# First two expert pairs gathered together as float32r halves, and three expert weight items asked for earlier

## The reference

```python
grp_prob = jax.nn.softmax((t @ w_grp) + b_grp, axis=-1)
g_prob, g_sel = lax.top_k(grp_prob, 1)                     # one of 4 groups
exp_logits = ((t @ w_rtr) + b_rtr).reshape(-1, N_GROUPS, EXP_PER_GROUP)
in_grp = jnp.take_along_axis(exp_logits, g_sel[:, :, None], axis=1)[:, 0]
e_prob, e_sel = lax.top_k(jax.nn.softmax(in_grp, axis=-1), 2)   # two of its 8 experts
gate = g_prob * e_prob / jnp.sum(e_prob, -1, keepdims=True)
...
hid = jax.nn.silu(jnp.einsum('td,edf->tef', t, w1)) * jnp.einsum('td,edf->tef', t, w3)
y = jnp.einsum('tef,efd->td', hid * combine[..., None], w2)
```

## Time and profile before

| | |
|---|---|
| median of 3 runs | 1316.39 us (1315.42 to 1318.79) |
| profiled execution, its own time | 1315.97 us |
| its span | 1314.2 us |
| TensorE busy | 97% of the span |
| mean granted TensorE clock | 0.992 of full |
| layer 0, experts | about 583 to 812 us of the span |
| layer 1, experts | about 1078 to 1302 us of the span |

### The profile page before, as it was taken

The page is one execution under the profiler, slowest core; times in us unless marked ns, Lnnn a source line. Parts: engine busy times, 40 slices in busy tenths (PEclk is TensorE's granted clock), DMA queues, the critical chain, the costliest instruction groups (busy, mean ns, idle before and its releaser), DMA issues.

```text
span 1314.2 us, 19284 instructions
## 1 busy us (share of the span) xinstructions
PE 1278.9 (97%) x7509; PEld 824.9 (63%) x7509; DVE 562.1 (43%) x1226; ACT 485.4 (37%) x1062; POOL 115.3 (9%) x167
## 2 busy tenths in 40 slices
PE   8999999999999999999999998999999999999996
PEld 7888588885888877454344443788887554444432
DVE  3325223262577584342232215678485242222224
ACT  3346333462663236212223323563235412223232
POOL 0000000000014331000000000004422000000000
PEclk9999999999999999989999999999999999999999
DMA  9753162332421234759999999231132859999994
GB/s 368 149 176 121 40 266 97 129 111 81 166 106 63 77 111 161 288 198 362 418 420 422 421 416 404 78 128 67 65 128 98 321 213 398 420 420 422 422 420 189
DMA packets 48847, 307.51 MB, mean 234 GB/s; under 512 B 5897, under 2 KB 6409, under 8 KB 16752
## 3 DMA queue, kind: packets, MB, share of 16 engines
q1 hardware_dynamic: 43760, 288.61, 55.3%
q0 software_dynamic: 3200, 8.16, 2.8%
q10 hardware_dynamic: 1792, 9.43, 1.9%
HBM read 301.17 MB, written 8.59 MB: 236 GB/s over the span
## 4 chain that ended last, share of the span: by engine, by line
PE 85%; DVE 10%; ACT 4%; issue 1%; DMA 0%; DVEq 0%; ACTq 0%; SPq 0%
PE ps L1136 25%; PE ps L1812 17%; PE ps L1839 9%; PE ps L1401 4%; PE ps L1176 4%; PE ps L1881 2%; PE ps L1902 2%; PE ps L1108 2%; PE ps L1621 1%; PE ps L1144 1%; DVE projT L2755 1%; DVE small L2754 1%; PE ps L1821 1%; PE ps L1611 1%; DVE projT L2746 1%
## 5 line engine op out<-in xcount | busy, mean ns | idle before, releaser
L1136 PE MATMUL ps<-hT,ring 128*128 128x272 f32 (+1 forms) x1840 | 437.1, 391 | 0.6 <-ACT hT L1995 0.6
L1136 PEld LDWEIGHTS ps<-hT,ring 128*128 128x128 f32 x1840 | 343.7, 191 | 66.2 <-issue 8.0
L1812 PE MATMUL ps<-ring,arena 128*64 128x512 f32 x416 | 139.3, 600 | 0.0
L3110 DVE TENSOR_TENSOR xo<-ps,xo 128x512 fp32r<-128x512 f32 x64 | 42.9, 689 | 99.5 <-ACT xo L2427 99.4
L3227 POOL TENSOR_TENSOR arena<-projT,cst 32x272 f32<-32x272 f32 x104 | 71.5, 687 | 114.2 <-DVE projT L2733 101.1
L1812 PE MATMUL ps<-projT,arena 128*64 128x512 f32 x240 | 80.0, 597 | 0.0
L3101 DVE TENSOR_TENSOR arena<-arena,ps 128x256 f32<-128x256 f32 x32 | 13.5, 421 | 140.6 <-ACT arena L2414 140.0
L1812 PEld LDWEIGHTS ps<-ring,arena 128*64 128x64 f32 x416 | 40.4, 137 | 51.9 <-issue 51.0
L2412 ACT ACTIVATE arena<-ps 128x256 f32<-128x256 f32 x32 | 12.3, 384 | 138.7 <-PE ps L1812 138.7
L2154 ACT ACTIVATE projT<-ps 128x272 f32<-128x272 f32 x68 | 27.0, 397 | 90.8 <-PE ps L1136 85.2
L1401 PE MATMUL ps<-ring,projT 128*128 128x512 f32 x128 | 56.6, 596 | 0.0
(11 more groups left out here) (511 smaller groups left out, 2026.6 us busy)
## 6 DMA issues: line engine op xcount, KB each, us to landing
ring<-experts SPq DMA_DIRECT2D x72, 1024.0 KB, 16.5
ring<-w_in SPq DMA_DIRECT2D x62, 1024.0 KB, 5.0
projT<-experts SPq DMA_DIRECT2D x48, 1024.0 KB, 15.8
arena<-experts SPq DMA_DIRECT2D x22, 1024.0 KB, 12.3
prm<-experts SPq DMA_DIRECT2D x22, 1024.0 KB, 16.0
ring<-w_out SPq DMA_DIRECT2D x16, 1024.0 KB, 4.8
spare<-experts SPq DMA_DIRECT2D x12, 1024.0 KB, 14.5
lent<-experts SPq DMA_DIRECT2D x8, 1024.0 KB, 10.2
```

The source lines that it names most:

```text
L1136: mm = pe.matmul(ps[:, chunk_bank(blk, l, j), 0:ncols], w[:, j % 2, k, :], hT[:, k, T - ncols:T], start=(k == 0), stop=(k == KC - 1))
L1812: mm = pe.matmul(ps[64 * e:64 * e + 64, 0, :], xg[:, 4 * h + k, i % 2, 64 * e:64 * e + 64], w[e][:, k // 2, 512 * (k % 2):512 * (k % 2) + ...
L3110: v.tensor_tensor(low, ps[:, 4 + half, :], high, ALU.subtract).then_inc(s("pair_rows_copied"), 1)
```

## The change

Pairs 0 and 1 are gathered by `gather_two(0, 0)` and `gather_two(0, 1)` before the first `up_half`; `gather_pair` is gone. Its second half goes to PSUM banks 6 and 7, so it does not wait for the copy of the first. VectorE builds `psel` in two parts of 256 columns rather than 128 and 384, and splits the first group's rows right behind, in two halves of 512 columns. `keep_busy` gets one more matmul of 512 columns in each layer. SyncE no longer waits for `rows_fetched` at item 14.

```diff
@@ SyncE
                     if j == 7 + MORE_SLOTS + ITEMS_WO:
                         sp.wait_ge(layer_normed, normed_at[l, 1, 2, 1])
-                        sp.wait_ge(rows_fetched, 16 * (GROUPS * l + 1))
@@
-        def together(i):
-            return i >= 2
         def copies_of(i):
-            return 2 * (min(i + 1, 2) + max(i // 2, 0))
+            return 2 * (i // 2 + 1)
+        def gather_bank(i, half):
+            return 6 if i == 0 and half else 2
@@ TensorE
-                    return group + 3 if group else 1 if q == 0 else 2
+                    return group + 3 if group else 1 if q < 2 else 2
...
-                def gather_pair(i):
-                    q = i % PAIRS_A_GROUP
-                    pe.wait_ge(s("pairs_selected"), selected(0, q))
-                    if i == 0:
-                        pe.wait_ge(rows_fetched, 16 * (GROUPS * l + 1))
-                    else:
-                        pe.wait_ge(s("pair_tokens_copied"), copies_of(i - 1))
-                    for k in range(KC):
-                        mm = pe.matmul(ps[:, 2 + k // 4, (k % 4) * P:(k % 4 + 1) * P], xrows[:, k * P:(k + 1) * P],
-                                       whole(psel)[:, 2 * q:2 * q + 2, :], start=True, stop=True)
-                        if k % 4 == 3:
-                            mm.then_inc(s("pair_gathered"), 1)
                 def gather_two(i, half):
                     q = i % PAIRS_A_GROUP
                     if half == 0:
                         pe.wait_ge(s("pairs_selected"), selected(i // PAIRS_A_GROUP, q))
-                        pe.wait_ge(s("rows_split"), i // PAIRS_A_GROUP + 1)
                         if q == 2:
                             pe.wait_ge(s("pairs_turned_copied"), i // PAIRS_A_GROUP + 1)
-                    pe.wait_ge(s("pair_tokens_copied"), copies_of(i - 1) + half)
+                    pe.wait_ge(s("rows_split"), i // PAIRS_A_GROUP + 2 if i else half + 1)
+                    if i:
+                        pe.wait_ge(s("pair_tokens_copied"), copies_of(i - 1) + half)
...
                 def experts_grouped():
-                    gather_pair(0)
+                    gather_two(0, 0)
+                    gather_two(0, 1)
...
                         if i == 0:
                             gate_slots(0)
-                            gather_pair(1)
...
-                keep_busy(4, *([256] if l < LAYERS - 1 else [384, 512, 512, 384]))
+                keep_busy(4, *([256, 512] if l < LAYERS - 1 else [384, 512, 512, 384, 512]))
@@ ScalarE: every pair of pairs by the 128x1024 copy, pairs 0 and 1 too
-                            if i == 0 or i % 2 and i + 1 < PAIRS:
+                            if i % 2 and i + 1 < PAIRS:
                                 tokens_in(i + 1)
@@ VectorE
-                        chosen(0, 2).then_inc(s("pairs_selected"), 1)
-                        chosen(2, PER_GROUP).then_inc(s("pairs_selected"), 1)
+                        chosen(0, 4).then_inc(s("pairs_selected"), 1)
+                        chosen(4, PER_GROUP).then_inc(s("pairs_selected"), 1)
...
                     v.wait_ge(rows_fetched, 16 * (GROUPS * l + g + 1))
-                    if g == 0:
-                        v.wait_ge(s("pair_gathered"), 4)
-                    VP(v.tensor_copy(rows_high, xrows))
-                    v.tensor_tensor(rows_low, xrows, rows_high, ALU.subtract).then_inc(s("rows_split"), 1)
+                    parts = [slice(0, 512), slice(512, D)] if g == 0 else [slice(0, D)]
+                    for c in parts:
+                        VP(v.tensor_copy(rows_high[:, c], xrows[:, c]))
+                        v.tensor_tensor(rows_low[:, c], xrows[:, c], rows_high[:, c], ALU.subtract).then_inc(s("rows_split"), 1)
...
                         hidden(i)
-                        if i == 0:
-                            split_rows(0)
...
                 select_pairs(0)
+                split_rows(0)
```

More of the change, by code:

```diff
@@ L1880, in gather_two @@
                         for part, rows in enumerate((rows_high, rows_low)):
-                            mm = pe.matmul(ps[:, 2 + k // 2, (k % 2) * 2 * P:(k % 2 + 1) * 2 * P], rows[:, c],
+                            mm = pe.matmul(ps[:, gather_bank(i, half) + k // 2, (k % 2) * 2 * P:(k % 2 + 1) * 2 * P], rows[:, c],
                                            psel[:, 2 * q:2 * q + 4, :], start=(part == 0), stop=(part == 1))
@@ L1885, in turn_pairs @@
                 def turn_pairs(g):
-                    pe.wait_ge(s("pairs_selected"), selected(g, 1))
+                    pe.wait_ge(s("pairs_selected"), selected(g, 2))
                     for q in range(PAIRS_A_GROUP):
@@ L2391, in tokens_in @@
                             a.wait_ge(s("pair_gathered"), copies_of(i) - 1 + half)
-                            if together(i):
-                                a.activation(xg[:, 4 * half:4 * half + 4].rearrange("p (b k) c n -> p b (k c n)", b=2),
-                                             ps[:, 2:4, :], ACT.Copy)\
-                                    .then_inc(s("pair_tokens_copied"), 1)
-                            else:
-                                a.activation(xg[:, 4 * half:4 * half + 4, i % 2, :],
-                                             ps[:, 2 + half, :].rearrange("p (k n) -> p k n", k=4), ACT.Copy)\
-                                    .then_inc(s("pair_tokens_copied"), 1)
+                            b = gather_bank(i, half)
+                            a.activation(xg[:, 4 * half:4 * half + 4].rearrange("p (b k) c n -> p b (k c n)", b=2),
+                                         ps[:, b:b + 2, :], ACT.Copy)\
+                                .then_inc(s("pair_tokens_copied"), 1)
                     def turned_in():
```

## The result

Over 22 runs of each in turn, the changed kernel took 1319.99 us in the median (1316.06 to 1324.09), the kernel before 1316.63. The ratio is 1.0025, 95% interval 1.0016 to 1.0033: **3.3 us slower**. That lies inside the predicted range and under the 3.9 us taken as the bound of "the same", but it is surely not the -0.2 us of the sum. The profiled execution took 1317.62 us, the second fastest of the 22; its span is 1315.8.

What follows compares the result with a forecast made beforehand. The prediction took TensorE, busy 97% of the span, as the bound. Layer 0 at -1.15 and layer 1 at +0.95 gave -0.2 us together: median 1316.2 us, range 1312.8 to 1320.8.

Steps and rivals of the forecast that it cites:

- layer 0, start: Layer 0's experts through `up_half(0, 0)`: added filling shortens the low-clock stretch to about 3 us, -0.8 us.
- layer 0, pair 1: Layer 0 ahead of `up_half(1, 0)`: gather removed, most of its time becomes idle, -0.35 us.
- layer 1, start, by the gather: Layer 1's start through `up_half(0, 0)`: longer filling and gather in halves start it later, +1.3 us.
- layer 1, start, by the items: Layer 1's store and fetch of rows beside three early weight items: shared evenly, cost 0.
- layer 1, pair 1: Layer 1 ahead of `up_half(1, 0)`: gather removed, most of its time becomes idle, -0.35 us.
- Part 3: TensorE ahead of pair 1: of the removed 2.03 us gather, 0.35 gained per layer, some 1.7 become idle.
- The rival: Behind `gate_slots(0)`, both layers: new idle time drops the clock, 1.5 or 3 us each, 1319.2 or 1322.2; chance 0.13.
- Part 5: SyncE's three weight items issued 12.8 us earlier: no reader waits, store and items share evenly, cost 0.
- The third rival: Late rows: early items delay store and fetch, +1.2 us in layer 1, 1317.4; chance 0.07.
- Part 1: VectorE before the first gather: half a cast takes 0.43 us and half a subtraction 0.69.
- Part 2: The gather itself and its filling, to `up_half(0, 0)`: layer 1 +1.3 us, layer 0 -0.8 us.
- Part 4: Later split of rows gone and ScalarE's copies changed: moved work is covered, nobody waited for it.

Runs made afterwards that it cites:

- e3: The changed kernel with two more filling matmuls (512 and 384 columns) behind `gate_slots(0)`; ratio to the kernel before 1.0019.
- e2: The changed kernel with SyncE's wait for the first fetch put back, leaving the gather part and longer filling; ratio to the kernel before 1.0023.
- i1: Second set of the kernel before with only SyncE's wait for the fetch taken away (early items alone); ratio to the kernel before 1.0011.
- g1: The changed kernel with SyncE's wait for the fetch put back and without the added 512-column filling matmul in both layers; ratio to the kernel before 1.0022.
- h1: The kernel before with the added 512-column filling matmul in layer 0 alone; ratio to the kernel before 0.9996.
- e4: The changed kernel with SyncE waiting at item 14 for the store of the normed rows, not the fetch; ratio to the kernel before 1.0032.
- h2: The changed kernel with the fetch wait put back, pair 1's gap filled, and the added filling in layer 0 only; ratio to the kernel before 1.0006.
- i2: Second set of the changed kernel with SyncE's wait for the first fetch put back (gather part alone); ratio to the kernel before 1.0015.
- g4: The changed kernel with SyncE's wait put back and pair 1's idle time filled by two matmuls (512 and 384 columns); ratio to the kernel before 1.0013.
- g2: The kernel before with one weight item instead of three going out early, the other two waiting for the fetch; ratio to the kernel before 1.0001.
- e1: The kernel before with only SyncE's wait for the fetch taken away (early items alone); ratio to the kernel before 1.0019.
- g3: The kernel before with pair 1 gathered as float32r halves, the split and `turn_pairs(0)` moved ahead for it; ratio to the kernel before 0.9998.

## Why the prediction was wrong

The time came from five terms. The sizes are those of the table, against before:

| term | predicted | measured |
|---|---|---|
| layer 0, start | -0.8 | -1.4 (mean of 7 profiles with gather and added filler) |
| layer 0, pair 1 | -0.35 | +1.4 to +1.6 |
| layer 1, start, by the gather | +1.3 | +1.3 |
| layer 1, start, by the items | 0 | +0.65 and +0.96 alone, +1.2 beside the gather (e3 less e2) |
| layer 1, pair 1 | -0.35 | -0.26, or +1.4 where the clock falls (2 of 5) |
| sum | -0.2 | +3.0 with 2 falls in 5; the runs' ratio gives +3.3 |

The last column adds up as -1.4 + 1.5 + 1.3 + 1.2 + 0.4 (the last is 3 times -0.26 and 2 times +1.4, over 5). That it comes so near to 3.3 is in part luck, since part of the -1.4 is chance (below, under "Right").

The runs' averages give the same picture another way: of the 3.3 us, 2.8 are at full clock (1306.7 against 1303.9). Worked out from the stretches, as an estimate, they are +2.5 in layer 1's start, +0.9 in layer 0's (-0.8 with 1.7 less lost to the low level) and -0.4 in the two pairs 1, in all 3.0. The falls in pair 1 (1.7, and 0.7 on average) and the shorter low stretch in layer 0 (-1.7) nearly cancel. Two steps failed.

**Part 3, the gather of pair 1.** The mechanism was right, to the idle time itself (1.79 and 1.62 for "some 1.7"), and the gain of removing the gather is 0.1 in layer 0 and 0.26 in layer 1, not 0.35 (the 0.14 us between VectorE's end and TensorE's start, "issue" in the chain above, was left out). What failed is the judgement that the clock would stay up. I took the one earlier case of 1.79 us of idle time at 1.00 as evidence, with the remark that the work around pair 1 is denser. In layer 0 that was wrong every time. The rival named it with place and price (1.5 for one fall), at 0.13, and counted on both layers; one fall in layer 0, sometimes a second, is what came. The Trainium skill, page "TensorE: Matmul & The Clock Gate", section "Part 1: The HAM clock gate", says that the throttled state is the default and activity lifts it; the falls here agree, while the 1.79 us of rows 7 show that an idle time of this length doesn't always bring one. What sets the two apart isn't shown.

**Part 5, the three items.** "If store and items share evenly, the store lands before 1072.09 and the cost is 0, which I take." It landed at 1063.75 + 8.5 = 1072.25, and behind three items it took 8.5 where alone it took 2.6. What failed is the overlap that the step assumed: sharing does come, but only 4.1 us behind the store's issue, and then at 0.52 MB beside 1.14 in 4.1 us. The limit was wrong as well: 1072.09 is the fetch's issue, and the store must land some 0.95 us ahead of it. The third rival had the other end (1074.5, +1.2 in layer 1, 0.07). Its price came true, with a fetch 2.5 us late and +1.2 beside the gather, but not its mechanism: the store doesn't stand behind all three. In i1 the third item, issued at 1065.07, lands 3.7 us after the store, issued at 1065.50 (DMA issues of i1, layer 1):

```profile
cst<-experts SPq DMA_DIRECT2D x1, 1024.0 KB, 12.2
normed_rows<-res ACTq DMA_DIRECT2D x1, 512.0 KB, 8.1
```

That the price fits is partly luck, also since the rival's terms as written (1063.7, 8.8, 1.2) add up to 1073.7 and not 1074.5. The Trainium skill, page "DMA: Bandwidth & Descriptors", section "Queues, rings and completion order", has each engine go round its queues a packet at a time. The packets from 1068 to 1072 agree, 143 of the store beside 244 of the items; the 4.1 us without one packet of the store are not what I took from it. It was that rule, and no row, that decided my choice of an end.

**Right.** Part 1, to 0.01 us. Part 2 in layer 1: +1.3, of it 0.9 the filler (g1). In layer 0 the mechanism (the filler shortens the low stretch) is right and shown by h1. Where the stretch lies as I put it (e2, e4, h2) the start is 0.7 to 0.8 shorter, as predicted; in three profiles (the change, e3, i2) there is none, and it is 2.0 to 2.3 shorter. The mean with g4 (1.5 shorter) is 1.4. Part of that is chance: in e3, i2 and g4 the low stretch at 576 to 579, which lies ahead of everything that the change adds, is missing too. Part 4 cost nothing that the stretches show. The item tried alone found no reader that waited (g2), and the wait at the end of layer 1 stayed.

**What stays open.** The early items alone cost 1.4 to 2.5 us by the ratios and 0.65 to 0.96 in the stretches of their profiles; the other stretches of those two profiles don't show the rest. One profile is one execution, and the ratio's interval reaches down to it. And the changed kernel lost 11.6 us (+-0.9) to the low clock where e2 and i2, with the same gather and filling, lost 12.8 (+-1.1); that can be chance. Why the store's and the fetch's first packets come late beside the items is open too.

## What to carry to other kernels

A matmul that can be made cheaper may be the cover of a wait: here its removal gave back 0.1 to 0.3 of 2 us, and the idle time was followed by a fall of the clock worth 1.7, each time in layer 0. If the work must go, fill the gap (e3, g4). A transfer without a reader is free only if nothing small and urgent goes to memory behind it: look how much time such a transfer has (6.0 us here) and how many bytes were asked for just before it: one 1 MB load left enough, three did not. And put a longer filler where the engine waits anyway (layer 0) but not where it is the filler itself that the next step waits for (layer 1, 0.9 us).

## What was unexpected in the hardware

- A 0.5 MB store on ScalarE's queue, issued 0.4 us behind the last of three 1 MB loads on SyncE's queue, took 8.1 to 9.1 us (the change, e1, i1, e3, both layers); alone 2.6 to 2.8; behind one load 5.5 and 6.2. Its first packet started 3.9 to 5.0 us behind the issue, 0.84 alone and 2.6 behind one load; from there on it moved beside the loads.
- The clock fell behind 1.79 us of idle time each time in layer 0 (5 of 5), and behind 1.62 us in layer 1 in 2 of 5. Every low stretch was 3.4 or 6.8 us long in all fourteen profiles, but for the one at the very end (from about 1306 on).
- Float32r matmuls of 128 columns, each with weights of its own, followed each other at 0.11 us (g3), those of 256 columns in `gather_two` at 0.12. Half the columns cost as much, so one pair gathered in halves (1.82) is hardly cheaper than in float32 (2.03).
